# Half-loads at a layer's start, and the shared expert's products split over two octets

## The reference

```
aff  = sigmoid(x @ w_router)                  # 64 experts, 8 groups, top 4 groups, top 8 experts
h    = silu(xb @ w_gate[e]) * (xb @ w_up[e])  # xb: the tokens that chose expert e; hidden 256
y    = h @ w_down[e]                          # scaled by the gate and added to the token
f    = sum over experts + (silu(x @ ws_gate) * (x @ ws_up)) @ ws_down   # one shared expert
x    = layer_norm(alpha * x + f)
```

## Time and profile before

| | |
|---|---|
| median of 3 executions | 1185.61 us (1185.02 to 1186.21) |
| the profiled execution | 1186.9 us, its span 1185.2 us |
| PE busy | 1151.6 us, 97% of the span |
| DVE, ACT, POOL busy | 347.2, 300.6, 56.4 us |
| DMA | 449.12 MB, 379 GB/s over the span |
| PE's granted clock, mean | 0.996 |

### The profile page before, as it was taken

One profiled execution on the slowest core, in us unless ns is written; L12 is line 12 of the kernel. 1 busy time (PEld: TensorE's weight loads), 2 busy tenths in 40 slices (PEclk: granted clock), 3 DMA queues, 4 the chain that ended last, 5 costly groups with the idle time before them and its releaser, 6 DMA issues.

```text
span 1185.2 us, 22166 instructions
## 1 busy us (share of the span) xinstructions
PE 1151.6 (97%) x8851; PEld 687.6 (58%) x8851; DVE 347.2 (29%) x912; ACT 300.6 (25%) x713; POOL 56.4 (5%) x100
## 2 busy tenths in 40 slices
PE   9999999999999999999999999999999899999995
PEld 6865755555555555554787647555555555555552
DVE  0445512222122222121523557221222222121224
ACT  1454222212121212121213533121222212121222
POOL 1431100000001000000011001000000010000000
PEclk9999999999999999999999999999999999999998
DMA  9945999999999999999980558999999999999995
GB/s 375 418 159 180 356 416 417 427 429 427 428 429 413 427 427 427 428 427 418 414 358 3 225 231 343 413 418 427 429 429 427 430 420 426 428 427 427 427 424 202
DMA packets 39613, 449.12 MB, mean 379 GB/s; under 512 B 4337, under 2 KB 4721, under 8 KB 10225
## 3 DMA queue, kind: packets, MB, share of 16 engines
q1 hardware_dynamic: 38816, 443.30, 89.6%
q10 hardware_dynamic: 720, 4.73, 1.0%
HBM read 446.96 MB, written 1.05 MB: 378 GB/s over the span
## 4 chain that ended last, share of the span: by engine, by line
PE 85%; DMA 9%; DVE 4%; issue 1%; ACT 1%; DVEq 0%; SPq 0%; ACTq 0%
PE bank L1266 18%; PE bank L1289 17%; PE bank L1323 17%; PE bank L818 8%; PE bank L837 6%; PE bank L1331 5%; PE bank L876 4%; DMA store<-in_w_gate 4%; DMA store<-in_w_down 3%; DMA store<-in_w_in_b 2%; PE bank L1296 2%; PE bank L1163 1%; PE bank L1033 1%; PE bank L1044 1%; DVE work L1695 1%
## 5 line engine op out<-in xcount | busy, mean ns | idle before, releaser
L1266 PE MATMUL bank<-store,work 128*64 128x256 f32 x1984 | 227.8, 382 | 3.0 <-DMA store<-in_w_gate 3.0
L1289 PE MATMUL bank<-store,work 128*64 128x256 f32 x1952 | 225.1, 379 | 5.1 <-issue 5.1
L1323 PE MATMUL bank<-store,work 128*32 128x512 f32 x1888 | 218.4, 595 | 0.5 <-DMA store<-in_w_down 0.3
L1266 PEld LDWEIGHTS bank<-store,work 128*64 128x64 f32 x1984 | 137.0, 137 | 115.1 <-issue 43.6
L1289 PEld LDWEIGHTS bank<-store,work 128*64 128x64 f32 x1952 | 143.3, 137 | 75.4 <-issue 8.4
L1983 DVE SCALAR_TENSOR_TENSOR yhalf<-bank,gcol,yhalf 128x512 fp32r<-128x512 f32 x124 | 93.0, 750 | 212.6 <-ACT yhalf L1617 212.6
L1617 ACT ACTIVATE yhalf<-bank,gcol 128x512 fp32r<-128x512 f32 x124 | 85.4, 689 | 181.4 <-PE bank L1323 181.4
L1975 DVE TENSOR_TENSOR work<-work,bank 128x256 f32<-128x256 f32 x64 | 27.0, 421 | 346.2 <-PE bank L1289 346.2
L1323 PEld LDWEIGHTS bank<-store,work 128*32 128x32 f32 x1888 | 56.1, 109 | 118.8 <-issue 110.7
L1455 ACT ACTIVATE work<-bank 128x512 f32<-128x512 f32 (+4 forms) x177 | 78.0, 441 | 100.7 <-PE bank L818 47.4
L1455 ACT ACTIVATE back<-bank 128x128 fp32r<-128x128 bf16 x64 | 17.8, 278 | 279.9 <-PE bank L1236 279.9
(11 more groups left out here) (185 smaller groups left out, 823.6 us busy)
## 6 DMA issues: line engine op xcount, KB each, us to landing
store<-in_w_gate SPq DMA_DIRECT2D x60, 2048.0 KB, 15.9
store<-in_w_down SPq DMA_DIRECT2D x56, 2048.0 KB, 17.1
store<-in_w_up SPq DMA_DIRECT2D x54, 2048.0 KB, 17.6
store<-in_w_up SPq DMA_DIRECT2D x14, 1024.0 KB, 9.1
store<-in_w_in_b SPq DMA_DIRECT2D x3, 3072.0 KB, 23.0
store<-in_w_out SPq DMA_DIRECT2D x4, 2048.0 KB, 14.2
store<-in_w_down SPq DMA_DIRECT2D x6, 1024.0 KB, 10.5
home<-in_w_gate SPq DMA_DIRECT2D x4, 1024.0 KB, 16.9
```

Source lines behind the costliest of these rows:

```text
L1266: last = pe.matmul(gate_bank[slots_of(e), 0:HID], xg[:, k, slots_of(2 * j + e)], w[e][:, k, :], start=(k == 0), stop=(k == KT - 1))
L1289: last = pe.matmul(up_bank[slots_of(e), 0:HID], xg[:, k, slots_of(2 * j + e)], w[e][:, k, :], start=(k == 0), stop=(k == KT - 1))
L1323: last = pe.matmul(yb[half][rows_of(t, e), :], hT[b][:, f, slots_of(e, t)], w[e][:, f, half * 512:half * 512 + 512], start=(f == 0), stop= ...
```

## The change

1. `gather_bank` ends in 1 in place of 2: chunk 7 follows chunk 4 in its bank.
2. In units 0 and 1 the gate product signals when half its k steps are done (`half_gated`), and in unit 1 the up product does too (`half_hidden`). SP loads the gate weights of pairs 2 and 3 and the up weights of pair 3 in two halves (1 MiB each, four of eight k steps for both experts), the first when half the product is done. The products of those units wait for both.
3. In unit 1, down(0) is done ahead of turn_h(1).
4. Octet 3 (`TURN_OCTET`) is written out. It does both turnings (units 0 and 1), down 0 in unit 2 and down 1 in unit 3. Octet 6 does down 2 in its unit 1 and down 3 in its unit 2. ACT's copies of the turned rows move with the turnings.
5. Semaphores that were made once per layer (`kept_..`, `gate_apart`, `shared_wd_landed`) are one for both, waited on with (l + 1) * 16.

```diff
@@ -55,6 +55,7 @@
 RES_OCTET = RES_PAIR // OCT_PAIRS
+TURN_OCTET = RES_OCTET - 1
 SHARED_OCTET = OCTETS - 2
@@ -254,7 +255,7 @@
 up_bank, gate_bank = banks[2], banks[3]
-gather_bank = (0, 1, 2, 0, 1, 2, 0, 2)
+gather_bank = (0, 1, 2, 0, 1, 2, 0, 1)
 first_gather_bank = (0, 2, 1, 3, 0, 1, 2, 0)
@@ -502,6 +503,29 @@
+def block_halves(l, part, i, b):
+
+    dst = matrices(matrix_at(b, 0, part), 2).rearrange("p (e k n) -> p e k n", e=2, k=KT)
+    src = (w_gate, w_up)[part][l, UNROLL * i + b].rearrange("p e (k n) -> p e k n", k=KT)
+    return [(dst[:, :, ks, :], src[:, :, ks, :]) for ks in (slice(0, KT // 2), slice(KT // 2, KT))]
+
+def reload_gate_halves(l, units, i, b):
+
+    halves = block_halves(l, 0, i, b)
+    sp.wait_ge(sem(f"half_gated_{l}"), units)
+    sp.dma_start(*halves[0]).then_inc(sem(f"gate_first{b}"), 16)
+    sp.wait_ge(sem(f"gated_{l}"), units)
+    sp.dma_start(*halves[1]).then_inc(sem(f"gate_landed{2 * b}_{l}"), 16)
+
+def reload_up_halves(l, units, i, b):
+
+    halves = block_halves(l, 1, i, b)
+    sp.wait_ge(sem(f"half_hidden_{l}"), 1)
+    sp.dma_start(*halves[0]).then_inc(sem("up_first"), 16)
+    sp.wait_ge(sem(f"hidden_{l}"), units)
+    sp.sem_inc(sem(f"up_landed{2 * b + 1}_{l}"), 16)
+    sp.dma_start(*halves[1]).then_inc(sem(f"up_landed{2 * b}_{l}"), 16)
+
 def reload(l, units, i, b, kept=False):
@@ -610,17 +634,18 @@
 filled(sp, G[l, "logit1"])
-sp.dma_start(matrices(matrix_at(1, 0, 0)), w_gate[l, 1, :, 0, :]).then_inc(sem(f"gate_apart_{l}"), 16)
+sp.dma_start(matrices(matrix_at(1, 0, 0)), w_gate[l, 1, :, 0, :]).then_inc(sem("gate_apart"), 16)
 used(sp, (l, "shared"))
 sp.dma_start(matrices(matrix_at(1, 1, 0)), w_gate[l, 1, :, 1, :]).then_inc(sem(f"gate_landed{UNROLL}_{l}"), 16)
 keep(l, 1, 1)
 sp.wait_ge(sem("xhi"), TT * (l + 1))
 sp.wait_ge(sem("xlo"), XLO * (l + 1))
 keep(l, 2, 0)
-reload_gate(l, 1, 1, 0)
+reload_gate_halves(l, 1, 1, 0)
 sp.wait_ge(sem(f"hidden_{l}"), 1)
 expert(l, 1, 1, 1)
-reload(l, 2, 1, 1)
+reload_gate_halves(l, 2, 1, 1)
+reload_up_halves(l, 2, 1, 1)
 reload_down(l, 1, 1, 0)
@@ -1250,10 +1275,12 @@
 if place == 1:
-    pe.wait_ge(s_("gate_apart"), 16)
+    pe.wait_ge(sem("gate_apart"), (l + 1) * 16)
+if place in (2, 3):
+    pe.wait_ge(sem(f"gate_first{b}"), (l + 1) * 16)
 for e in range(2):
     if kept:
-        pe.wait_ge(s_(f"kept_0{e}"), 16)
+        pe.wait_ge(sem(f"kept_0{e}"), (l + 1) * 16)
 w = [gate_view(b, e) for e in range(2)]
@@ -1265,6 +1292,8 @@
                          start=(k == 0), stop=(k == KT - 1))
+    if place < 2 and k == KT // 2 - 1:
+        last.then_inc(s_("half_gated"), 1)
 last.then_inc(s_("gated"), 1)
@@ -1275,19 +1304,23 @@
     if kept:
-        pe.wait_ge(s_(f"kept_1{e}"), 16)
+        pe.wait_ge(sem(f"kept_1{e}"), (l + 1) * 16)
 w = [up_view(b, e) for e in range(2)]
 if kept:
     w = [resident_view(1, e) for e in range(2)]
 if place == 0:
     pe.wait_ge(s_("up_apart"), r * 16 + 16)
     w[0] = up_apart
+if place == 3:
+    pe.wait_ge(sem("up_first"), (l + 1) * 16)
 for k in range(KT):
     if by_halves and k == KT // 2:
         pe.wait_ge(s_(f"up_landed{2 * b + 1}"), rs * 16 + 16)
     for e in range(2):
         last = pe.matmul(up_bank[slots_of(e), 0:HID], xg[:, k, slots_of(2 * j + e)], w[e][:, k, :],
                          start=(k == 0), stop=(k == KT - 1))
+    if place == 1 and k == KT // 2 - 1:
+        last.then_inc(s_("half_hidden"), 1)
 last.then_inc(s_("hidden"), 1)
@@ -1365,13 +1398,13 @@
-def unit(r, o, j, place=3, last=False, kept=False, kept_before=False, shared=None):
+def unit(r, o, j, place=OCT_PAIRS, last=False, kept=False, kept_before=False, turn=None, turned=None, add=None):
     O = r * OCTETS + o
     U = O * OCT_PAIRS + j
     b = j % 2
     rs = 2 * O + j // 2
-    if shared in (1, 2):
-        pe.wait_ge(sem(f"shared_hT_{l}"), r * TT + (shared + 1))
+    if turned is not None:
+        pe.wait_ge(sem(f"shared_hT_{l}"), r * TT + (turned + 2))
     gate(U, O, j, rs, kept, place)
@@ -1388,15 +1421,17 @@
 turn_back(U + 1, OCTET * o + 2 * j + 2, 1 - b)
+if place == 1:
+    down(U - 1, 1 - b, 2 * O, O + 1, U + 2, False, False)
 turn_h(U)
-if shared in (0, 1):
-    shared_turn(shared, r)
-for q in ((), (0,), (1, 2), (3,))[shared or 0]:
-    shared_down(q, r)
+if turn is not None:
+    shared_turn(turn, r)
+if add is not None:
+    shared_down(add, r)
 ahead = j == OCT_PAIRS - 1
 if ahead:
     gather(O + 1, U + 2)
-if place > 0:
+if place > 1:
     down(U - 1, 1 - b, 2 * O + (j - 1) // 2, O + 1 + ahead, U + 2, kept_before, place == 2)
@@ -1404,16 +1439,18 @@
     unit(r, 0, j, place=j)
-with pe.Fori(1, RES_OCTET) as o:
+with pe.Fori(1, TURN_OCTET) as o:
     for j in range(OCT_PAIRS):
         unit(r, o, j)
+for j in range(OCT_PAIRS):
+    unit(r, TURN_OCTET, j, turn=(0, 1, None, None)[j], turned=(None, 0, 1, None)[j], add=(None, None, 0, 1)[j])
 for j in range(OCT_PAIRS):
     unit(r, RES_OCTET, j, kept=(j == 0), kept_before=(j == 1))
 with pe.Fori(RES_OCTET + 1, SHARED_OCTET) as o:
     for j in range(OCT_PAIRS):
         unit(r, o, j)
 for j in range(OCT_PAIRS):
-    unit(r, SHARED_OCTET, j, shared=j)
+    unit(r, SHARED_OCTET, j, add=(None, 2, 3, None)[j])
 for j in range(OCT_PAIRS):
@@ -1662,11 +1699,14 @@
     unit(r, 0, j, first=(j == 0))
-with act.Fori(1, SHARED_OCTET) as o:
+with act.Fori(1, TURN_OCTET) as o:
     for j in range(OCT_PAIRS):
         unit(r, o, j)
 for j in range(OCT_PAIRS):
-    unit(r, SHARED_OCTET, j, shared=j)
+    unit(r, TURN_OCTET, j, shared=j)
+with act.Fori(TURN_OCTET + 1, OCTETS - 1) as o:
+    for j in range(OCT_PAIRS):
+        unit(r, o, j)
 for j in range(OCT_PAIRS):
...
```

More of the change, by code:

```diff
@@ L526, in keep @@
                 w = (w_gate, w_up, w_down)[part][l, RES_PAIR, :, e, :]
-                sp.dma_start(resident_view(part, e), by_f(w) if part == 2 else by_k(w)).then_inc(sem(f"kept_{part}{e}_{l}"), 16)
+                sp.dma_start(resident_view(part, e), by_f(w) if part == 2 else by_k(w)).then_inc(sem(f"kept_{part}{e}"), 16)
             rows = [[(biasrow[:], router_bias.rearrange("(o a) b -> o a b", o=1).broadcast_to([P, DEPTH, NE])),
@@ L596, in _ @@
                 sp.wait_ge(sem("softened"), sum(len(jobs[i]) for i in range(l + 1)))
-                sp.dma_start(shared_wd, by_row_pair(ws_down[l])).then_inc(sem(f"shared_wd_landed_{l}"), 16)
+                sp.dma_start(shared_wd, by_row_pair(ws_down[l])).then_inc(sem("shared_wd_landed"), 16)
                 used(sp, (l, "out0"))
@@ L1159, in shared_down @@
                     t, half = q // 2, q % 2
-                    pe.wait_ge(sem(f"shared_wd_landed_{l}"), 16)
+                    pe.wait_ge(sem("shared_wd_landed"), (l + 1) * 16)
                     pe.wait_ge(sem(f"shared_hT_{l}"), r * TT + (t + 2))
@@ L1307, in down @@
                         elif kept:
-                            pe.wait_ge(s_(f"kept_2{e}"), 16)
+                            pe.wait_ge(sem(f"kept_2{e}"), (l + 1) * 16)
                             w.append(resident_view(2, e))
```

## The result

The changed kernel takes 1189.84 us (median of 7, 1188.96 to 1193.27) beside 1185.72 us for the kernel before (7 runs, 1185.02 to 1186.35). The ratio is 1.0038, 95% interval 1.0029 to 1.0048: slower by 0.38%, outside the range that was given, and on the other side of what was forecast as likeliest. The profiled execution took 1189.21 us with a span of 1187.5, so it shows 2.3 us of the loss: 0.3 lie ahead of layer 0's unit 0, 0.6 between it and layer 1's unit 0, and 1.4 behind that. Of the other six runs two lie 0.2 us lower and four 0.6 to 4 us higher, and no trace shows where those went.

The account below looks back on a forecast made before the run. The weights' DMA queue, not PE, was taken to bound each layer's end. Gains at the load after the kept pair, 0.7 us in layer 0 and 0.0 in layer 1, gave 1185.6 - 0.7 = 1184.9 us; range 1181.2 to 1187.6.

Parts of the forecast that it names:

- What bounds the kernel: Whole layer: each layer's end is the end of the weights' byte stream; PE time saved after unit 16 buys nothing.
- rival D: Whole kernel: PE was the bound after all, so some 9.4 us would be won, 1176.2 us; chance 0.03.
- Half-loads: Layer start, 135 to 150 us: early halves fill the queue's hole; load before 184.42 lands 2.5 us earlier.
- Rival E: Half-loads: each pays its own start of 3.0 us, 18 us in all, 1203.6 us; chance 0.01.
- What the first hole leaves: Down load at 184.42, after the first gather: bound by PE's release, it keeps 1.4 us of the early gain.
- g: Gain at the down load of 184.42: 9.2 + 0.7 - L, taken as 1.4 us.
- L: Time to landing of a load meeting a queue about empty: rows 7.7 to 9.2 us, taken as 8.5.
- The shared expert: Octet 3: the down in unit 15 costs 1.4 us net, paid by g, so what follows moves by 0.
- Rival B: Unit 15's down product starves the queue: 1187.7 us at L = 9.2, deciding from L = 9.3; chance 0.13.
- my own formula: Load after the kept pair, both layers: gains (9.2 - 1.4 + g - L) + (8.5 - 1.4 + g - L), 0.7 us at L = 8.5.
- Code loading: Written-out octet 3: four more code packets a layer, 0.3 us if spread; bad end 4.9 us, 1189.8, chance 0.04.
- Down before turning, and the gather's bank: Unit 1 and gathers: PE 0.41 us earlier and 0.3 us per gather; buffer for load 184.42 freed 0.7 us earlier.

Follow-up runs that it names:

- halves_late: Kernel before with half-loads alone, both halves issued only when the whole product is done: ratio 1.0040, 1191.04 us.
- pe_edits_only: Kernel before with only the gather's bank change and down before turning in unit 1: ratio 1.0011, 1186.57 us.
- unrolled_only: Kernel before with octet 3 written out on PE and nothing else changed: ratio 1.0014, 1187.74 us.
- unrolled_three: Kernel before with octets 1, 2 and 3 written out on PE, no other change: ratio 1.0032, 1191.27 us.
- shared_only: Kernel before with the shared expert's split alone, octet 3 written out for it, down 1 in unit 15: ratio 1.0027, 1189.15 us.
- two_in_15: shared_only with both downs of octet 3 in unit 15, none in unit 14; against the kernel before: ratio 1.0045, 1193.06 us.

## Why the prediction was wrong, step by step

**What bounds the kernel: right.** Each layer's end is the end of the queue. PE was 2.9 us ahead of before at unit 28 and had to wait at units 29 to 31; rival D's 9.4 us never came. The 3 to 4 us of waits predicted there appeared: 3.9.

**Half-loads, "2.5 us earlier at the load before 184": the step that failed first.** It measured 1.8 and 0.9 us later in the changed kernel. I had priced a half at 0.1 us from a single one that stood behind 17 us of queue; the other three of that kind in the same trace took 0.1, 0.1 and 0.4 more than their bytes. At the layer's start three loads in halves of 4 KB pieces cost 3 us (halves_late), and the early start returned about 2. Rival E had the right direction with a wrong mechanism and a price three times too high (9 us a layer): it isn't a start paid by every DMA, since 8 KB runs in as many DMAs lost nothing.

**"What the first hole leaves", g = 1.4.** It was to be g = 9.2 + 0.7 - L with the load bound by PE's release. Released 0.75 us earlier, it landed only 0.2 to 0.35 us earlier (pe_edits_only), and on average over all kernels 0.2. g in the changed kernel was -0.7 and -0.1. The rows that I took for an empty queue (7.9 and 7.7) weren't that either: the load ahead of each landed 1.6 and 1.8 us after their issue.

**The shared expert, "all that follows moves by 1.4 - g = 0": the step that decided the sign.** The price of the product in unit 15, 1.4 us, was right: the kept pair's gate is 1.4 and 1.65 us later after unit 0. What should have paid for it, g, wasn't there. Rival B is what happened, with another cause: I had it decide by a slow landing (L of 9.3 or more), and it decided at L = 8.6 and 8.0, since g was missing. The time to landing that I took for uncertain was nearly the low end of my bounds: 7.7 to 7.8 us into a queue about dry. With the measured g and L of the changed kernel my own formula gives -(9.2 - 1.4 - 0.7 - 8.6) - (8.5 - 1.4 - 0.1 - 8.0) = 2.5 us slower, where the profiled run has 2.3. That agreement is luck. The formula has this load landing 1.5 and 1.0 us later and it landed 0.7 and 1.1 later; the lost g didn't pass to unit 15's up product in layer 0 (201.4 us after unit 0, it was 201.3); and before and after alike the load lands 4.9 to 5.1 us behind the one ahead of it, so the slowest part of the queue never ran dry there. What the hole costs shows in the GB/s behind the kept pair (386 in place of 407) and not in this one load.

**Code loading, "0.3 us if spread" with 4% for worse: mis-sized.** One octet written out, seven more packets in the whole run, cost 1.7 us (0.6 to 2.7), three, with fifteen more, 3.8 us (2.5 to 5.1). That is 0.2 to 0.3 us a packet; spread evenly a packet would be 0.04 and at the worst, as I had it, 0.6, though a packet took 1.05 us on average. The Trainium skill ("Runtime: NRT & Kernel Launch", Instruction fetch mechanics) calls the refill of straight code mostly hidden; PE indeed shows no stall of its own, but the kernel is slower. In unrolled_only's layer 0 the delay is one part's of sixteen, which fits with the unchanged GB/s; in unrolled_three it is most parts'. That a code packet made them late is argued and wasn't shown.

**Down before turning, and the gather's bank: right** in their 0.4 and 0.3 us of PE time, and right to be worth nothing beyond the queue.

The parts measured alone add up: 0.9 us for the halves, 1.7 for the written-out octet, 1.5 for the place of the two downs (shared_only less unrolled_only), 0 to 1.3 for PE's edits; in all 4.1 to 5.4, against 4.5 by the ratio. Each has an uncertainty of 1 us, and the 1.5, a difference of two, of about 1.5; by the double dose (two_in_15 less unrolled_only, 3.7 us) the place of the downs is clear of it. Open stays why PE's edits alone measured 0.6 us over before by the median, and why single runs differ: those of the changed kernel by 4 us, those of before by 1.3 beside it and by 2 to 5 in the later sessions.

## What to carry to other kernels

Where two limits lie on top of each other, ask of each edit which of the two it touches: work moved to where PE waits is free only up to the last wait ahead of the point where PE must be on time, here the product before the pair that needs no load. A load cut in two starts earlier, but its pieces get shorter, and with 4 KB pieces on a short queue that cost at least what the start gained; price a piece by several rows of its size, and try its form alone. Writing a loop out wasn't free here, where the weights' queue is the bound: its code comes over the same engines, and one octet cost 0.14%. A landing is that of the last of sixteen parts, so a sum over single landings follows one straggler; compare the GB/s of the stretch and the landings of several kernels too.

## What the runs showed of the hardware that was not expected

Three loads of 2 MiB, each cut into two DMAs of 4 KB pieces, cost 3 us more behind a short queue, with the engines' share at 1.01 and only 390 GB/s; with 8 KB pieces they cost nothing, though the early start didn't reach a landing either. A 4 KB piece kept its engine 177 ns, a 16 KB piece 618. Written-out code cost about 0.2 to 0.3 us for each 16 KB packet at an unchanged 427 GB/s. The sixteen parts of one load land 2.6 us apart by the median of the kernel before, and up to 6.0, and the last one sets the landing. And a 2 MiB load into a queue about dry landed after 7.7 to 7.8 us, 4.9 of them, by 429 GB/s, for its bytes.
